# A hybrid encoder layer: the mixer's output projection in two passes over the tokens, with seven weight blocks kept in SBUF

## The reference, cut to what matters

```
c   = RMSNorm_pre(x) @ w_in                      # projections of both branches, and two gates
A   = RWKV-7 time mixing;  Bd = differential attention
mix = sigmoid(g_a) * (A @ w_out_a) + sigmoid(g_b) * (Bd @ w_out_b)
x   = x + RMSNorm_post(mix @ w_o)                # w_o is 1024 x 1024
x   = x + RMSNorm_post_ffn((silu(h @ w_ug) * (h @ w_uv)) @ w_ffn_out),  h = RMSNorm_pre_ffn(x)
```

## Time and profile before

| | |
|---|---|
| median of 3 runs | 1100.82 us (1100.54 to 1101.74) |
| the profiled execution | 1105.81 us, its span 1104.0 us |
| PE busy | 1022.2 us (93%) |
| DVE, ACT, POOL busy | 496.6, 275.5, 489.9 us |
| wo blocks 1 to 7 | 613.2 to 659.3 us |
| norms and pair 0 of the feed-forward | 659.3 to 699.0 us |
| feed-forward loop, down projection, last norm | 699.0 to 1104.0 us |

### The profile page before, as it was taken

The page is one execution under the profiler, slowest core; times in us unless marked ns, Lnnn a source line. Parts: engine busy times, 40 slices in busy tenths (PEclk is TensorE's granted clock), DMA queues, the critical chain, the costliest instruction groups (busy, mean ns, idle before and its releaser), DMA issues.

```text
span 1104.0 us, 21751 instructions
## 1 busy us (share of the span) xinstructions
PE 1022.2 (93%) x8886; PEld 962.7 (87%) x8886; DVE 496.6 (45%) x859; ACT 275.5 (25%) x768; POOL 489.9 (44%) x327
## 2 busy tenths in 40 slices
PE   4999998899889999899989995999999999999994
PEld 4999998887678787788789994999999999999994
DVE  5566798367666455544257217233332333200003
ACT  4223452255533132231221234111110110010111
POOL 3556564323224114223065450565555655556561
PEclk8999999899979999999699996999999999999997
DMA  7232233412113110003312621223232332332232
GB/s 240 75 95 77 77 77 97 120 59 64 55 41 84 31 31 31 31 31 112 106 50 71 192 81 39 69 84 95 76 95 83 88 95 76 88 89 87 74 85 82
DMA packets 137581, 89.15 MB, mean 81 GB/s; under 512 B 5243, under 2 KB 129505, under 8 KB 137505
## 3 DMA queue, kind: packets, MB, share of 16 engines
q1 hardware_dynamic: 128356, 70.42, 22.5%
q10 hardware_dynamic: 9148, 17.65, 4.5%
HBM read 78.86 MB, written 9.19 MB: 80 GB/s over the span
## 4 chain that ended last, share of the span: by engine, by line
PE 76%; DVE 15%; issue 3%; ACT 3%; DMA 2%; POOL 1%; ACTq 1%; DVEq 0%; SPq 0%; POOLq 0%
PE dense L900 62%; PE side L952 3%; DVE amax L1515 1%; PE side L826 1%; DMA mb<-gates 1%; DVE qkv L1531 1%; PE side L852 1%; ACT qkv L1175 1%; PE side L816 1%; PE side L1072 1%; DVE otok L1542 1%; DVE mb L1809 1%; PE side L806 1%; DVE gt L1636 1%; PE side L766 1%
## 5 line engine op out<-in xcount | busy, mean ns | idle before, releaser
L655 POOL TENSOR_SCALAR w_hi<-w_raw 128x1024 fp32r<-128x1024 f32 x127 | 138.7, 1092 | 449.7 <-PE dense L900 431.7
L900 PE MATMUL dense<-h_hi,w_hi 128*128 128x272 f32 x1392 | 307.1, 298 | 10.9 <-DVE h_lo L1451 9.4
L658 POOL TENSOR_TENSOR w_lo<-w_raw,w_hi 128x1024 fp32r<-128x1024 f32 x127 | 311.8, 2455 | 10.6
L900 PE MATMUL dense<-h_hi,w_lo 128*128 128x272 f32 x1392 | 297.6, 292 | 0.0
L900 PE MATMUL dense<-h_lo,w_hi 128*128 128x272 f32 x1392 | 297.0, 291 | 0.0
L900 PEld LDWEIGHTS dense<-h_hi,w_hi 128*128 128x128 f32 x1392 | 224.6, 192 | 22.3 <-DVE h_lo L1451 10.3
L900 PEld LDWEIGHTS dense<-h_lo,w_hi 128*128 128x128 f32 x1392 | 225.6, 192 | 0.0
L900 PEld LDWEIGHTS dense<-h_hi,w_lo 128*128 128x128 f32 x1392 | 224.0, 192 | 0.0
L900 PE MATMUL dense<-S,w_hi 128*128 128x272 f32 x960 | 161.9, 291 | 1.8 <-DVE S L1812 1.6
L900 PEld LDWEIGHTS dense<-S,w_hi 128*128 128x128 f32 x960 | 136.4, 189 | 2.6 <-DVE S L1812 2.0
L900 PE MATMUL dense<-S,w_lo 128*128 128x272 f32 x480 | 99.5, 289 | 0.0
(11 more groups left out here) (248 smaller groups left out, 1327.2 us busy)
## 6 DMA issues: line engine op xcount, KB each, us to landing
w_raw<-in_w_ffn_in SPq DMA_DIRECT2D x44, 512.0 KB, 3.8
w_raw<-in_w_in SPq DMA_DIRECT2D x43, 512.0 KB, 3.9
w_raw<-in_w_ffn_out SPq DMA_DIRECT2D x16, 448.0 KB, 3.6
gates<-gst ACTq DMA_DIRECT2D x16, 272.0 KB, 2.0
w_raw<-in_w_o SPq DMA_DIRECT2D x8, 512.0 KB, 3.8
w_raw<-in_w_ffn_out SPq DMA_DIRECT2D x8, 512.0 KB, 3.7
mb<-gates ACTq DMA_DIRECT2D x1, 2176.0 KB, 10.6
ga<-gates ACTq DMA_DIRECT2D x1, 2176.0 KB, 10.3
```

What stands on the lines that cost most here:

```text
L655: nc.gpsimd.tensor_scalar(w_hi[:, slot, :], w_raw[:, slot, :], 1.0, 0.0, ALU.mult, ALU.add).then_inc(hi_split, 1)
L658: nc.gpsimd.tensor_tensor(w_lo[:, slot, :], w_raw[:, slot, :], w_hi[:, slot, :].bitcast(F32), ALU.subtract).then_inc(w_split, 1)
L900: ins = pe.matmul(acc[:, hf, 0:HALF], w, r[:, hf * HALF:(hf + 1) * HALF], start=first and n == 0, stop=final and n == 2)
```

## The change

The tokens of the projection `w_o` are cut at token 256: LATE is tiles 2, 3 and 4 (288 tokens), EARLY tiles 0 and 1 (256 tokens). `woA` i is block i for the late tokens, 24 matmuls of 288 columns; `woB` i is the same block for the early ones, 24 of 256. All `woA` come first. The split weights of seven of the eight blocks stay in SBUF from pass A to pass B, in the part of `S` (slices 8 to 21) that only the feed-forward loop fills; block 5's stay in a `w_hi`/`w_lo` slot. `unit(u)` of such a block waits for the end of `outA` 0 (blocks 0 to 4) or of `outA` 7 (blocks 6 and 7), not for a slot.

`zw` takes the place of `ztok` for the two passes: three transposes in pass A, two in pass B, into one side bank, with two buffers `zTs` instead of one `zT`. The norm steps of the late tiles are put among the blocks of pass B, in the list `late`. Those of tiles 0 and 1 come after it, and the late half of `ug` 0 and `uv` 0 stands among them. ACT's square in `zB` writes to `z` in SBUF and no longer to a PSUM bank of `dense`. Pair 0's first steps on ACT and DVE are cut at token 256 too. `S` lies at another address. The loop and the down projection have the same instructions as before.

```
-DENSE += [(k, i) for k in ("gB", "gA", "outB", "outA", "wo") for i in range(8)]
+DENSE += [(k, i) for k in ("gB", "gA", "outB", "outA", "woA", "woB") for i in range(8)]
...
+    elif _kind == "woB":
+        SEGS.append((next(u for u, w in enumerate(UNITS) if w[:2] == ("woA", _i)), _kind, _i))
...
+LATE, EARLY = [2, 3, 4], [0, 1]
+RANK = {t: n for n, t in enumerate(LATE + EARLY)}
+WO_PART = {"A": (2 * P, TOK - 2 * P, LATE), "B": (0, 2 * P, EARLY)}
...
-    for r, kind in enumerate(("wo", "down")):
-        for i in range(8):
-            s += [dense(kind, i)] + ([("ztok", r, i - 1)] if i else [])
-        s += [("ztok", r, 7), ("zS", r)]
-        s += first_pair(skew(NT, "zA0", "zB", "zC"), [("ug", 0), ("uv", 0)]) + [("ffn",)] if r == 0 else [("zA1", t) for t in range(NT)]
+    late = [[("zS", 0, "A")], [("zA0", 2), ("zA0", 3), ("zB", 2)], [("zA0", 4), ("zB", 3), ("zC", 2)], [("zB", 4), ("zC", 3)], [("zC", 4)]]
+    for i in range(8):
+        s += [dense("woA", i)] + ([("zw", "A", i - 1)] if i else [])
+    for i in range(8):
+        s += [dense("woB", i), ("zw", "B", i - 1) if i else ("zw", "A", 7)] + (late[i] if i < len(late) else [])
+    s += [("zw", "B", 7), ("zS", 0, "B"), ("zA0", 0), ("zA0", 1), ("zB", 0), ("dense", "ug", 0, 0, BY_TOKENS), ("zB", 1)]
+    s += [("dense", "uv", 0, 0, BY_TOKENS), ("zC", 0), ("zC", 1)]
+    s += [("dense", "ug", 0, 1, BY_TOKENS), ("dense", "uv", 0, 1, BY_TOKENS), ("ffn",)]
+    for i in range(8):
+        s += [dense("down", i)] + ([("ztok", 1, i - 1)] if i else [])
+    s += [("ztok", 1, 7), ("zS", 1, "")] + [("zA1", t) for t in range(NT)]
     return s
...
+Z_SUMS = {(0, "A"): (0, ((P, 2, SAMPLE), (DEC, SAMPLE, NT))), (0, "B"): (2, ((P, 0, 2),)),
+          (1, ""): (3, ((P, 0, SAMPLE), (DEC, SAMPLE, NT)))}
...
+    zTs = sb("zTs", [P, 2, TOK - 2 * P])
+    zT = zTs[:, :, :].rearrange("p a n -> p (a n)")[:, 0:TOK]
     gain2 = sb("gain2", [P, D])
     h2_hi = sb("h2_hi", [P, KT, TOK], F32R)
     h2_lo = sb("h2_lo", [P, KT, TOK], F32R)
+    sb("s_pad", [P, 288])
+    S = sb("S", [P, FT, 2, TOK], F32R)
+    wo_sb = S[:, 8:FT, :, :].rearrange("p a b n -> p (a b n)")[:, 0:14 * D].rearrange("p (j q n) -> p j q n", q=2, n=D)
...
+        def split(slot, hi):
+            nc.gpsimd.tensor_scalar(hi, w_raw[:, slot, :], 1.0, 0.0, ALU.mult, ALU.add).then_inc(hi_split, 1)
+
+        def split_lo(slot, hi, lo):
+            nc.gpsimd.tensor_tensor(lo, w_raw[:, slot, :], hi.bitcast(F32), ALU.subtract).then_inc(w_split, 1)
 
         def unit(u):
+            kind, i, _ = UNITS[u]
             pool.wait_ge(raw_loaded[u % 2], 16 * (u // 2 + 1))
-            if u >= 2:
-                pool.wait_ge(seg_done, UNIT_END[u - 2])
-            split(u % 2)
+            if kind == "woA" and i != 5:
+
+                pool.wait_ge(seg_done, BLOCK_END[("outA", 0 if i < 5 else 7)])
+                hi, lo = wo_sb[:, i - (i > 5), 0, :], wo_sb[:, i - (i > 5), 1, :]
+            else:
+                hi, lo = w_hi[:, u % 2, :], w_lo[:, u % 2, :]
+                if u >= 2:
+
+                    v = next(v for v in range(u - 2, -1, -2) if UNITS[v][0] != "woA" or UNITS[v][1] == 5)
+                    pool.wait_ge(seg_done, UNIT_END[v])
+            split(u % 2, hi)
             pool.wait_ge(hi_split, u + 1)
-            split_lo(u % 2)
+            split_lo(u % 2, hi, lo)
...
-        def three(acc, whi, wlo, rhi, rlo, first, final, halves=(0, 1)):
+        def three(acc, whi, wlo, rhi, rlo, first, final, places=((0, 0, HALF), (1, HALF, HALF))):
 
             for n, (w, r) in enumerate(((whi, rhi), (whi, rlo), (wlo, rhi))):
-                for hf in halves:
-                    ins = pe.matmul(acc[:, hf, 0:HALF], w, r[:, hf * HALF:(hf + 1) * HALF],
-                                    start=first and n == 0, stop=final and n == 2)
+                for bk, t0, tn in places:
+                    ins = pe.matmul(acc[:, bk, 0:tn], w, r[:, t0:t0 + tn], start=first and n == 0, stop=final and n == 2)
             return ins
...
+                if kind == "c":
+                    landed(pe, ("normB", (2, SAMPLE)[part]), "n1")
+
+                    pe.wait_ge(s_["x_sq"], NT)
+                else:
+                    landed(pe, ("zC", (LATE, EARLY)[part][-1]), "n1")
...
-                    if kind == "wo" and i == 0:
+                    if kind == "woA" and i == 0:
                         pe.wait_ge(s_["mix_done"], n + 1)
                     if kind == "down" and i == 0:
                         pe.wait_ge(s_["f_lo"], DOWN_PARTS[p][0] + n + 1)
                     c, rh, rl = ops[n]
-                    ins = three(acc, w_hi[:, u % 2, c:c + P], w_lo[:, u % 2, c:c + P], rh, rl,
-                                p == 0 and n == 0, p == len(parts) - 1 and n == len(ops) - 1,
-                                (0, 1) if parts_ > 0 else (part,))
+                    hi, lo = w_hi[:, u % 2, c:c + P], w_lo[:, u % 2, c:c + P]
+                    if kind in ("woA", "woB"):
+                        if i != 5:
+                            hi, lo = wo_sb[:, i - (i > 5), 0, c:c + P], wo_sb[:, i - (i > 5), 1, c:c + P]
+                        places = [(0, *WO_PART[kind[-1]][0:2])]
+                    elif kind in ("ug", "uv"):
+                        places = [(1 - part, *WO_PART["AB"[part]][0:2])]
+                    else:
+                        places = [(hf, hf * HALF, HALF) for hf in ((0, 1) if parts_ > 0 else (part,))]
+                    ins = three(acc, hi, lo, rh, rl, p == 0 and n == 0, p == len(parts) - 1 and n == len(ops) - 1, places)
...
+            elif k == "zw":
+                _, part, i = step
+                block_landed(pe, ("wo" + part, i))
+                buf = zTs[:, (i + 8 * (part == "B")) % 2, :]
+                transposes(step, "z", [(q * P, buf[:, q * P:q * P + TILES[t][1]]) for q, t in enumerate(WO_PART[part][2])])
...
-                pe.wait_ge(s_["xnorm"], t + 1)
...
+            elif k == "zw":
+
+                _, part, i = step
+                b = full_bank(act, step, "z")
+                for q, t in enumerate(WO_PART[part][2]):
+                    n = TILES[t][1]
+                    ins = f_act(h2_lo[0:n, t, 0:P], b[0:n, q * P:(q + 1) * P], ACT.Square, accum_out=zsq[0:n, t, i:i + 1])
+                A.mark(ins, s_["z_sq"], "z_sq")
...
-                r = step[1]
-                for i, (n, a, b_) in enumerate(((P, 0, SAMPLE), (DEC, SAMPLE, NT))):
-                    act.wait_ge(s_["z_sum"], 2 * r + i + 1)
+                first_sum, pieces = Z_SUMS[step[1:]]
+                for i, (n, a, b_) in enumerate(pieces):
+                    act.wait_ge(s_["z_sum"], first_sum + i + 1)
...
-                act.wait_ge(s_["zres"], t + 1)
-                A(f_act(dps[0][0:n, :, :], x1[0:n, t, :].rearrange("p (a b) -> p a b", a=2), ACT.Square,
-                        accum_out=ssq[0:n, t:t + 1]))
+                act.wait_ge(s_["zres"], RANK[t] + 1)
+                A(f_act(z[0:n, t, :], x1[0:n, t, :], ACT.Square, accum_out=ssq[0:n, t:t + 1]))
                 A.mark(f_act(rms[0:n, t:t + 1], ssq[0:n, t:t + 1], ACT.Sqrt, scale=1.0 / D, bias=EPS), s_["xrms"], "xrms")
-                if t == SAMPLE:
+                if t == EARLY[-1]:
                     act.dma_start(gain[:, :], i_["norm_ffn_post"][0].partition_broadcast(P)).then_inc(s_["gain_loaded"], 16)
...
-                        s_["f_tanh"], 1)
+                    if before:
+                        f_act(f_t.rearrange("p (a b) -> p a b", a=2), pa[:, :, 0:HALF], ACT.Tanh, scale=0.5).then_inc(
+                            s_["f_tanh"], 1)
+                    else:
+                        f_act(f_t[:, 0:2 * P], pa[:, 0, 0:2 * P], ACT.Tanh, scale=0.5)
+                        f_act(f_t[:, 2 * P:TOK], pa[:, 1, 0:TOK - 2 * P], ACT.Tanh, scale=0.5).then_inc(s_["f_tanh"], 1)
...
+                    if kind != "down":
+                        _, n, tiles = WO_PART[kind[-1]]
+                        q = i + 8 * (kind == "woB")
+                        if q >= 2:
+
+                            full_bank(act, ("zw", "AB"[(q - 2) // 8], (q - 2) % 8), "z")
+                        f_act(zTs[:, q % 2, 0:n], acc[:, 0, 0:n], ACT.Copy).then_inc(block_sem(d), 1)
+                        continue
                     if i:
 
-                        full_bank(act, ("ztok", int(kind == "down"), i - 1), "z1")
+                        full_bank(act, ("ztok", 1, i - 1), "z1")
                     f_act(zT[:, :].rearrange("p (a b) -> p a b", a=2), acc[:, :, 0:HALF], ACT.Copy).then_inc(block_sem(d), 1)
...
+            elif k == "zw":
+                _, part, i = step
+
+                if (part, i) == ("A", 0):
+                    dve.wait_ge(s_["gain_loaded"], 16 * 2)
+                gi = gain[:, i * P:(i + 1) * P]
+                tiles = WO_PART[part][2]
+                dve.wait_ge(s_["z_sq"], i + 8 * (part == "B") + 1)
+                b = bank(step, "z")
+                if part == "A":
```

(50 more changed lines are left out.)

31 lines of the change are left out of this document (13 added, 18 removed).

## The result

| | before | after |
|---|---|---|
| median of 11 runs | 1101.16 us | 1095.83 us (1088.73 to 1098.71) |
| ratio | | 0.9936, 95% interval 0.9919 to 0.9954 |
| the profiled execution | 1105.81 us | 1088.73 us |
| ahead of outA | 577.8 | 568.4 |
| outA's start to ug 1 | 121.2 | 115.1 |

The kernel became 5.3 us faster by the medians and 7.0 by the ratio; 1093.8 was forecast. The profiled pair differs by 17.1 us, and that would mislead: 9.4 of it lie ahead of outA, where both kernels have the same instructions (see after_again and before_again). The change's own stretch, from outA's start to ug 1, is 6.1 us shorter; 7.3 was forecast. Behind ug 1 the kernel is 1.6 us shorter, where nothing was forecast.

The account below looks back on a forecast made before the run. PE bounds the kernel (busy 93% of the span, 76% of the chain); time is won where it stands, slows or waits. ug 1 moves from 699.0 to 691.7: 1100.82 - 7.3 = 1093.5, plus 0.3 for width: 1093.8; range 1088.5 to 1099.5.

Parts of the forecast that it names:

- Part 1: Weight splits moved into outA: DVE's port lock makes mix 3.6 to 4.5 us later, pass A's first transposes about 622.7.
- part 4: Behind the passes: tiles 0 and 1's norms covered by ug 0 and uv 0's late half; ug 1 at 691.7, not 699.01.
- Two signs: Clock 1.00 at ug 0's early half was expected; a changed 405 us from ug 1 to the end would refute the prediction.
- Its last term: Before pass A's first transposes: ACT's copy starts 5.53 us after A0 ends, held back by ACT's DMAs.
- The supply of weights: In pass A: POOL needs 3.9 us per weight unit, PE 3.5, but POOL is five units ahead, so weights don't bind.
- Part 2: The two passes: time goes by columns, 24 matmuls in 3.18 and 2.86 us; a floor at 256 columns would cost 1.3.
- Part 3: Late tiles beside pass B: 2.1 us of transposes, 2.6 wait at tile 2, 0.4 for tiles 3 and 4; ends 673.9.
- R2: Clock falls to 1.2 GHz at tile 2's wait and before ug 0's early half: 2 x 2.2 us, 1098.2; chance 0.18.
- R1: In outA: POOL's early splits cost DVE nothing at the port, mix ready as today, 4.4 us kept: 1089.4; chance 0.15.
- R3: In pass B: late tiles are late at every turn through ACT's order, 4.8 us more, 1098.6; chance 0.12.
- R4: In outA: DVE loses the port twice per period, mix ready some 13 us later, 1107; chance 0.10.
- The end: From ug 1 on, loop and down projection are the same instructions and keep their length of 405 us.

Follow-up runs that it names:

- after_again: The changed kernel run again without an edit, for a second trace: 1096.46 us, ratio 0.9943 to before.
- before_again: The kernel before the change run again without an edit, for a second trace: 1102.05 us, measured once.
- late_split: Changed kernel, but only block A0's weights are split early; blocks 1 to 4 wait for the end of outA 7: 1100.07 us, ratio 0.9975 to before.
- spread_split: Changed kernel with the edits of late_split and dma_spread together: 1089.81 us, ratio 0.9883 to before.
- all_five: spread_split plus zc_later's edit, 18 unused matmuls ahead of ug 0's early half and 19 within block A0: 1086.91 us, ratio 0.9856 to before.
- zc_later: Changed kernel with PE's transposes of the late tiles each one block of pass B later: 1092.48 us, ratio 0.9896 to before.
- dma_spread: Changed kernel with ACT's DMAs of second gain and x issued one by one behind the copies of A1 to A6: 1095.17 us, ratio 0.9919 to before.
- tr_long: Changed kernel with 4 and 60 unused transposes added behind tile 0's and tile 1's, ahead of ug 0's early half: 1100.56 us, measured once.

## Why the prediction was right

The time lies in the range and near the forecast, and the mechanism (norms of the late tiles beside pass B, paid for at the port) is what the experiments show. But that the number came so near is in part luck. Part 1 was 1.2 us too dear, part 4 was 2.1 us too cheap, and behind ug 1 the kernel became 1.6 us shorter, for which the prediction had no reason. Two signs that the prediction named against itself came true as well: the clock was not 1.00 at the early half of ug 0, and the length from ug 1 to the end changed. By steps, in us from outA's start, or as lengths:

| step | forecast | measured |
|---|---|---|
| residual 7 of mix ready | 37.9 to 38.8 | 38.1 (568.42 to 606.55) |
| pass A's first transposes | 44.9 | 43.7 |
| 24 matmuls of 288 and of 256 | 3.18, 2.86 | 3.20, 2.84 |
| wait at tile 2 | 2.6 | 2.56 |
| from pass A's first transposes to B7's | 51.8 | 52.12 |
| from B7's transposes to ug 1 | 17.2 | 19.3 |
| sum | 113.9 | 115.1 |
| from ug 1 to the end | 0 less | 1.6 less |

**Part 1** was right in the port: mix was ready 3.8 us later than before (38.1 against 34.3; 3.6 to 4.5 were forecast), and late_split shows the early splits as the cause, with 4.3 us. Its last term was too large by 1.2: ACT's seven DMAs took 3.85 us, from 607.73 to 611.58, and not 5.53. That would have given 1.7 us, and 1.2 came out, because A1 ran at 1.2 GHz and was itself the last to be ready. I had called A1 "done before, even at the low clock"; that was wrong by a little. In spread_split the low clock there costs some 2.5 us (40.46 against 37.94 in all_five, at full clock).

**The supply of weights** didn't bind, but the reason given (POOL five units ahead) left out that POOL would wait 10 us for loads that stand behind the tiles of x. A6's weights were ready 0.7 us before their use (626.02 and 626.71). That they were in time rested on a margin that I hadn't worked out, so it was luck.

**Part 2** was right: the time goes by columns, 3.20 and 2.84 us, and no floor shows at 256 columns.

**Part 3** was right to 0.3 us, the wait and its place included, and zc_later shows that only 0.74 us stood behind it.

**Part 4** was mis-sized, for the most part by what rival R2 had foreseen: the clock fell ahead of the early half of ug 0, and its 24 matmuls took 4.66 us in the chain of waits, against 3.13 in dma_spread, where it didn't fall. That is 1.5 of the 2.1 us. The other 0.6 are small excesses, in the start of the early half (10.9 us after B7's transposes, 10.7 forecast) and from it to ug 1 (6.9 against 6.5, both without a fall). R2 had the clock fall after both waits. In the five traces that have both waits and nothing added, it fell after one of them in four (after, after_again, dma_spread, spread_split) and after both in late_split. The price by the stretches is 1.3 to 1.5 us each, R2 had 2.2. A forecast with one such fall would have said about 1095.3. The reason given against R2 was that the gap without any work is short, 1.7 us at most. In tr_long the transposes didn't let the clock fall, so that part of the reason stands; but a gap of 1.64 us was enough in four of seven traces.

**The end.** The loop and the down projection were to have the same length. From ug 1 to the end the changed kernel and its variants take 402.8 to 403.5 us, the two traces of before 405.0. See the last section.

**R1, R3, R4** don't hold: DVE pays at the port in every period from 585.08 on, tiles 3 and 4 are in time, and each waiting DVE step ends behind the one POOL step that it met (the last two, 4.22 us together, met one each).
